# A reordered start: first weights ahead of the activations, the first norm inside the third chunk

## The chip, the cores and the metric

One core of a Trainium2 chip runs the whole program. The metric is the time of one execution on the device in microseconds (us), lower is better. The kernel before took 1706.38 us as the median of three runs (1705.44 to 1707.03).

The engines have their own instruction streams and meet only at semaphores: TensorE (PE in the profile, with its weight loads as PEld), VectorE (DVE), ScalarE (ACT), GpSimd (POOL), and SyncE (SP), which here only issues DMA transfers. Matrix products are written into eight banks of an accumulator memory (PSUM), which the kernel names PS (four banks) and AX (four banks).

## The reference, cut to what matters

The reference is one step of a two-layer streaming encoder over 512 prompt tokens and 32 sample tokens of 1024 features. What this change touches is the very first projection, and the first norm of the memory tokens:

```python
def _rmsnorm(x, g):
    xf = x.astype(jnp.float32)
    y = xf * lax.rsqrt(jnp.mean(xf * xf, axis=-1, keepdims=True) + EPS)
    return (y * g.astype(jnp.float32)).astype(x.dtype)

# layer 0, mixer:
z = _rmsnorm(x, p["g_mix"][l]) @ p["w_in_even"][e]      # (512 + 32, 1024) @ (1024, 2600)
a_b, a_c, a_x, b_q, b_k, b_v, i_q, i_k, i_w = _split(z, EVEN_SIZES)
# ... sparse attention, short convolution, output projection, cross-attention, gated FFN

# memory tokens (256), once per layer:
hm = _rmsnorm(mem, g)
k = _rmsnorm((hm @ w_k).reshape(bsz, m, X_HEADS, X_HEAD_DIM), k_norm)
v = (hm @ w_v).reshape(bsz, m, X_HEADS, X_HEAD_DIM)
```

All of it is float32, and the output has to agree with a float32 reference.

## The kernel before, in words

Everything is held feature-major: a tile is 128 features by 548 token columns (512 prompt, 4 unused, 32 sample), and eight such tiles make up x. To get float32 accuracy from rounded operands, each operand is split in two: a rounded high part (XH, WHI) and the remainder (XL, WLO). A product is then three passes, WHI by XH, WHI by XL and WLO by XH (`product`, L836), each over two halves of 274 columns.

Weights come in **chunks**, 128 output features by all 1024 input features (512 KB, tile WRAW, two buffers used in turn). For each chunk ScalarE rounds WRAW to WHI (`hi`, L448), GpSimd forms WLO = WRAW - WHI (`lo`, L407), and TensorE makes 8 steps (one per input tile, `k`) of six products (`chunk`). VectorE takes the result out of PSUM (`evict`, L1224), and the next chunk but one may then write there. SyncE loads a chunk's weights two chunks ahead, as soon as `lo` of the chunk that last used the buffer is done (semaphore `lo_done`).

The norm is not applied to x. The products run on x times the gain, and each eviction multiplies by RSTD, the reciprocal root of the mean square per token. For it ScalarE squares every x tile (SQ, L462), VectorE sums the eight (SQA, L1207), TensorE multiplies by a matrix of 1/1024 (`mean_square`, L879, into AX banks 0 and 1), ScalarE takes the root (`std`, L473) and VectorE the reciprocal (`rstd`, L1218). So nothing can be evicted before RSTD is there. The memory tokens have the same: a square of the whole 128x2048 tile (MSQ, L525), three halving adds (L1256 to L1258), a product (L926), a root (L534), a reciprocal (RM, L1269) and two transposes (L931) that bring it into RMC.

The first nine chunks of the phase `in_even` are called chunks 0 to 8 below. The order of each engine's instructions is written out by hand, with no planner:

- SyncE: all of the parameters (PR), x tiles 0 and 1, weights of chunk 0, x tiles 2 to 7, constants (CST), weights of chunk 1, CSTB, the memory tokens (MRAW), two small tables, and then, once `lo` of chunk 0 is done, the weights of chunk 2.
- ScalarE: for each x tile the rounding XH and the square SQ in turn; `hi` of chunk 0 after the second tile, `hi` of chunk 1 after the eighth, then MSQ, `hi` of chunk 2, `std`, `hi` of chunk 3.
- VectorE: for each x tile the remainder XL (L1202) and the sum SQA in turn, then the three adds of MSQ, RSTD, the eviction of chunk 0, RM, the evictions of chunks 1 and 2.
- TensorE: chunk 0, `mean_square`, the product of MSQ, chunk 1, chunk 2, the transposes of RM, chunk 3, two small products for the position bias (L937, L938), chunk 4.

From chunk 4 on each chunk has a group of index products of the sparse attention in its middle, and a head norm behind it; VectorE works on scores, head norms and top-k. Chunk 4's middle waits for tables that the steps above produce (`band_vec`, `ki_ready`).

## Time and profile before

| | before |
|---|---|
| median of 3 runs | 1706.38 us |
| the profiled execution's own time | 1706.99 us |
| its span, first to last instruction | 1705.2 us |
| mean granted TensorE clock | 0.982 |
| TensorE busy | 1621.0 us (95%) |
| VectorE, ScalarE, GpSimd busy | 998.2, 637.0, 633.6 us |
| first matrix product | 12.79 us after the span's start |

A timeline row gives the start of a group of like instructions, its length, the engine and line, what it writes and reads, how many there are (x2), and in brackets the idle time of the engine before it and what ended that. Lengths can overlap a little, so the distance from start to start is the safer price of an instruction in a sequence. The kernel is bound by TensorE over most of its length; the edit lies in the first 50 us.

### The profile page before, as it was taken

To read this page: it belongs to the slowest core of one execution; us is meant where nothing else is said; L and a number is where in the kernel's file an instruction comes from. 1 tells how busy PE (TensorE), PEld (TensorE's weight loads), DVE (VectorE), ACT (ScalarE), POOL (GpSimd) and SP (SyncE) were. 2 spreads that over 40 slices of the span, in tenths; PEclk is the share of its full clock that TensorE was granted. 3 is DMA by queue.
4 is the path that set the end of the run, shared out by engine and by line. 5 is a ranking of instruction groups with operands and counts; after the bars stand their busy time and mean duration, and the time that the engine had idled before them with its cause. 6 is when DMAs were issued, how large, how long until landed. Compare 5 with 4: busy or idle time off the path is not lost.

```text
span 1705.2 us, 30940 instructions
## 1 busy us (share of the span) xinstructions
PE 1621.0 (95%) x11888; PEld 1536.8 (90%) x11890; DVE 998.2 (59%) x1300; ACT 637.0 (37%) x960; POOL 633.6 (37%) x305
## 2 busy tenths in 40 slices
PE   5889977998999999999999979899899999999999
PEld 5789843997799999999999979799699999999999
DVE  6799965456355556455656879456646554045530
ACT  5343355335234332233334755333533333123320
...
DMA packets 41714, 153.50 MB, mean 90 GB/s; under 512 B 5344, under 2 KB 5856, under 8 KB 40360
## 3 DMA queue, kind: packets, MB, share of 16 engines
q1 hardware_dynamic: 41640, 152.46, 27.0%
...
q14 instruction: 21, 0.17, 0.0%
...
## 4 chain that ended last, share of the span: by engine, by line
PE 75%; issue 10%; POOL 5%; DVE 5%; ACT 4%; DMA 0%; POOLq 0%; DVEq 0%; SPq 0%; ACTq 0%
PE PS L836 68%; POOL WLO L407 5%; PE AX L1103 2%; DVE RB L1588 1%; PE AX L1012 1%; PE AX L1109 1%; PE AX L896 1%; ACT WHI L448 1%; PE AX L1040 1%; DVE RB L1590 1%; PE PS L1023 1%; ACT LG L632 1%; PE PS L1075 0%; DVE RSTD L1218 0%; DVE SQA L1236 0%
## 5 line engine op out<-in xcount | busy, mean ns | idle before, releaser
L407 POOL TENSOR_TENSOR WLO<-WRAW,WHI 128x1024 fp32r<-128x1024 f32 (+3 forms) x299 | 633.3, 2127 | 1054.1 <-ACT WHI L448 1054.1
L448 ACT ACTIVATE WHI<-WRAW 128x1024 fp32r<-128x1024 f32 (+3 forms) x299 | 268.8, 919 | 721.7 <-PE PS L836 663.6
L836 PE MATMUL PS<-XH,WHI 128*128 128x274 f32 x2256 | 479.9, 294 | 24.9 <-POOL WLO L407 18.4
L836 PE MATMUL PS<-XH,WLO 128*128 128x274 f32 x2256 | 475.7, 292 | 0.0
L836 PE MATMUL PS<-XL,WHI 128*128 128x274 f32 x2256 | 473.2, 291 | 0.0
L836 PEld LDWEIGHTS PS<-XH,WHI 128*128 128x128 f32 x2256 | 361.6, 191 | 33.0 <-POOL WLO L407 18.5
L836 PEld LDWEIGHTS PS<-XL,WHI 128*128 128x128 f32 x2256 | 360.4, 191 | 0.0
L836 PEld LDWEIGHTS PS<-XH,WLO 128*128 128x128 f32 x2256 | 360.0, 191 | 0.0
L836 PE MATMUL PS<-HH,WHI 128*128 128x274 f32 x1216 | 257.3, 293 | 0.7 <-DVE HL L1442 0.7
L836 PE MATMUL PS<-HH,WLO 128*128 128x274 f32 x1216 | 254.6, 291 | 0.0
L836 PE MATMUL PS<-HL,WHI 128*128 128x274 f32 x1216 | 254.4, 291 | 0.0
L836 PEld LDWEIGHTS PS<-HH,WHI 128*128 128x128 f32 x1216 | 194.1, 191 | 2.2 <-DVE HL L1442 1.1
L836 PEld LDWEIGHTS PS<-HL,WHI 128*128 128x128 f32 x1216 | 194.2, 190 | 0.0
L836 PEld LDWEIGHTS PS<-HH,WLO 128*128 128x128 f32 x1216 | 194.1, 191 | 0.0
L1453 DVE TENSOR_TENSOR X<-PS,X 128x548 f32 x56 | 40.8, 729 | 190.9 <-PE PS L836 190.9
L1202 DVE SCALAR_TENSOR_TENSOR XL<-X,PR,XH (+1 forms) x48 | 101.3, 2110 | 53.3 <-ACT XH L461 53.3
L1548 DVE TENSOR_TENSOR HL<-H,HH 128x548 f32 x44 | 87.6, 1992 | 41.0 <-ACT HH L701 41.0
L1539 DVE SCALAR_TENSOR_TENSOR YB<-GB,PR,YB 128x548 f32<-128x548 f32 x44 | 75.5, 1715 | 54.5 <-ACT YB L695 54.5
L1533 DVE TENSOR_TENSOR GB<-PS,RSTD 128x548 f32<-128x548 f32 x44 | 32.0, 728 | 79.6 <-PE PS L836 79.6
L698 ACT ACTIVATE GE<-YB 128x548 f32<-128x548 f32 x44 | 29.1, 662 | 121.2 <-DVE YB L1540 121.2
L1236 DVE RECIPROCAL SQA<-STD 128x548 f32<-128x548 f32 (+1 forms) x17 | 53.5, 3145 | 4.8 <-ACT STD L486 4.5
L1543 DVE TENSOR_TENSOR GE<-GE,RSTD 128x548 f32<-128x548 f32 x44 | 32.1, 730 | 32.0 <-ACT GE L698 32.0
...
## 6 DMA issues: line engine op xcount, KB each, us to landing
WRAW<-in_w_in_even SPq DMA_DIRECT2D x29, 512.0 KB, 3.7
WRAW<-in_w_up0a SPq DMA_DIRECT2D x22, 512.0 KB, 3.6
WRAW<-in_w_up0b SPq DMA_DIRECT2D x22, 512.0 KB, 3.7
WRAW<-in_w_up1a SPq DMA_DIRECT2D x22, 512.0 KB, 3.6
WRAW<-in_w_up1b SPq DMA_DIRECT2D x22, 512.0 KB, 3.6
WRAW<-in_w_mv SPq DMA_DIRECT2D x16, 512.0 KB, 3.6
WRAW<-in_w_xq SPq DMA_DIRECT2D x16, 512.0 KB, 3.6
WRAW<-in_w_xo SPq DMA_DIRECT2D x16, 512.0 KB, 3.7
```

Of the source, the lines that this page charges most:

```text
L407: pool.tensor_tensor(WLO[parity][:, first:last], WRAW[parity][:, first:last], WHIf[parity][:, first:last], ALU.subtract).then_inc(lo_done, ...
L448: act.activation(WHI[parity][:, first:last], WRAW[parity][:, first:last], ACT.Copy).then_inc(hi_done, 2 // len(cuts))
L698: act.activation(GE[:], YB[:], ACT.Gelu_apprx_tanh).then_inc(gelu_done, 1)
L836: ins = pe.matmul(dst, w, x, start=first, stop=last)
L1103: ins = pe.matmul(AX[:, 2 + d, :], MV[:, mb, P * (2 * u + d):P * (2 * u + d) + P], PTX[:, s % 2, mb, :], start=mb == 0, stop=mb == 1)
L1202: dve.scalar_tensor_tensor(XL[:, m, :], X[:, m, :], par(g, m + g0), XHf[:, m, :], ALU.mult, ALU.subtract).then_inc(xl_ready, 1)
L1236: dve.reciprocal(SQA[:, 0:cols], STD[:, 0:cols]).then_inc(std_read, 1)
L1453: dve.tensor_tensor(halves(X[:, m, :]), PS[:, (t0 + k) % 2, :, 0:H], halves(X[:, m, :]), ALU.add).then_inc(evicted, 1)
L1533: dve.tensor_tensor(halves(GB[:, 4:552]), PS[:, t0 % 2, :, 0:H], halves(RSTD[:]), ALU.mult).then_inc(evicted, 1)
L1539: link(dve.scalar_tensor_tensor(YB[:], GB[:, 3:551], par("f_w", f * 3 + (3 * q0 + 1)), YB[:], ALU.mult, ALU.add))
L1543: link(dve.tensor_tensor(GE[:], GE[:], RSTD[:], ALU.mult))
L1548: dve.tensor_tensor(HL[:, f, :], H32[:], HHf[:, f, :], ALU.subtract).then_inc(hl_ready, 1)
```

## The change

What it does, in the order of the engines:

- **SyncE.** The parameters are reordered and loaded in two pieces, a first of 73 columns (eps, the gains and the two cross-attention norms) and later the other 486. The weights of chunk 0 come right behind the first piece, ahead of all of x; the weights of chunk 1 behind x. The weights of chunk 2, with their wait for `lo_done`, move ahead of MRAW and the small tables.
- **Two pieces of the weights' roundings.** Chunks 0 and 1 join the set whose `hi` and `lo` are made in two halves of 512 columns, so TensorE can start a chunk after the first half of `lo`.
- **ScalarE.** A root of one column (WARM) comes first and takes the load of the root's table with it. Then `hi` of chunk 0, all eight XH, `hi` of chunk 1, then the eight SQ with `hi` of chunk 2 behind the third, then MSQ, `std`, `hi` of chunk 3.
- **VectorE.** All eight XL first, then all eight sums. The eviction of chunk 1 moves ahead of RM, that of chunk 2 too, which reads AX instead of PS.
- **TensorE.** Four products on zeros (L937 of the changed kernel, 128x512 in full float32) come first. Chunks 0, 1 and 2 follow one another; chunk 2 writes AX banks 2 and 3 and so waits for no eviction. `mean_square` comes after chunk 2's first step, the product of MSQ after chunk 2, into bank 0. Chunk 3 waits for two evictions, as before. The transposes move behind chunk 3, into bank 1.

```diff
-IN_HALVES = {*range(C0["in_even"] + EVEN_HEAD, C0["mv0"] + 8), *range(C0["odd"], C0["out_odd"] + 2)}
+IN_HALVES = {C0["in_even"], C0["in_even"] + 1, *range(C0["in_even"] + EVEN_HEAD, C0["mv0"] + 8), *range(C0["odd"], C0["out_odd"] + 2)}
...
-            sp.dma_start(PR[:], a["par"]).then_inc(par_landed, 16)
+            sp.dma_start(PR[:, 0:PAR_FIRST], a["par"][:, 0:PAR_FIRST]).then_inc(par_landed, 16)
+            load(0, a["w_in_even"][0], COLS[0], 0)
             for m in range(0, KT, 2):
                 sp.dma_start(X[:, m:m + 2, :], a["x"][:, m:m + 2, :]).then_inc(x_landed[m // 2], 16)
-                if m == 0:
-                    load(0, a["w_in_even"][0], COLS[0], 0)
+            load(1, a["w_in_even"][1], COLS[1], 1)
+            sp.dma_start(PR[:, PAR_FIRST:PAR_COLS], a["par"][:, PAR_FIRST:PAR_COLS]).then_inc(par_rest_landed, 16)
             sp.dma_start(CST[:], a["cst"]).then_inc(cst_landed, 16)
-            load(1, a["w_in_even"][1], COLS[1], 1)
             sp.dma_start(CSTB[:], a["cstb"]).then_inc(cst_landed, 16)
+            load(2, a["w_in_even"][2], COLS[2], 0)
             sp.dma_start(MRAW[:], a["mem"]).then_inc(mem_landed, 16)
             sp.dma_start(OH[:], a["onehot"]).then_inc(bias_in_landed, 16)
             sp.dma_start(RT[:], a["rel"]).then_inc(bias_in_landed, 16)
-            load(2, a["w_in_even"][2], COLS[2], 0)
...
             act.wait_ge(par_landed, 16)
+            act.activation(WARM[:], par("eps"), ACT.Sqrt)
+            hi(0, 0, COLS[0], 0)
             for m in range(KT):
                 if m % 2 == 0:
                     act.wait_ge(x_landed[m // 2], 16)
-                norm_tile(0, m, m % 2)
-                if m == 1:
-                    hi(0, 0, COLS[0], 0)
+                act.activation(XH[:, m, :], X[:, m, :], ACT.Copy, scale=par("g_mix", m)).then_inc(xh_ready, 1)
             hi(1, 1, COLS[1], 0)
+            for m in range(KT):
+                if m >= 2:
+                    act.wait_ge(sq_summed, m - 1)
+                act.activation(SQ[:, m % 2, :], X[:, m, :], ACT.Square).then_inc(sq_ready, 1)
+                if m == 2:
+                    ahead(c0)
+            act.wait_ge(par_rest_landed, 16)
             act.wait_ge(mem_landed, 16)
             act.activation(MSQ[:], MRAW[:], ACT.Square).then_inc(msq_ready, 1)
-            ahead(c0)
             std(0)
             ahead(c0 + 1)
...
-                if not isinstance(t, int) or t >= 2:
+                if not isinstance(t, int) or t >= 3:
                     pe.wait_ge(evicted, t - 1)
...
+                    dst = AX[:, 2:4, :] if isinstance(t, int) and t == THIRD_SLOT else PS[:, slot, :, :]
...
+            pe.wait_ge(warm_in, 1)
+            for i in range(4):
+                ins = pe.matmul(AX[:, 0, :], SQA[:, 0:P], SQA[:, 0:512], start=True, stop=True)
+            ins.then_inc(warm_out, 1)
             even_chunk(0)
+            even_chunk(1)
             pe.wait_ge(cst_landed, 32)
-            mean_square(0)
+            even_chunk(2, {1: lambda: mean_square(0)})
             pe.wait_ge(msum_ready, 1)
-            pe.matmul(AX[:, 2, 0:MEM], ONES_D, MSQ[:, 0, :], start=True, stop=True).then_inc(mssq_mm, 1)
-            even_chunk(1)
-            even_chunk(2)
+            pe.wait_ge(std_ready, 1)
+            pe.matmul(AX[:, 0, 0:MEM], ONES_D, MSQ[:, 0, :], start=True, stop=True).then_inc(mssq_mm, 1)
+            even_chunk(3)
             pe.wait_ge(std_read, 2)
...
-            even_chunk(3)
             pe.wait_ge(bias_in_landed, 32)
-            pe.wait_ge(rmc_ready, 1)
+            pe.wait_ge(evicted, 3)
...
-            zero_sum(0)
+            dve.memset(SQA[:], 0.0).then_inc(warm_in, 1)
             dve.memset(UB[:, 0:4], 0.0)
             dve.wait_ge(par_landed, 16)
+            for m in range(KT):
+                dve.wait_ge(xh_ready, m + 1)
+                dve.scalar_tensor_tensor(XL[:, m, :], X[:, m, :], par("g_mix", m), XHf[:, m, :], ALU.mult,
+                                         ALU.subtract).then_inc(xl_ready, 1)
+            dve.wait_ge(warm_out, 1)
+            for m in range(KT):
+                dve.wait_ge(sq_ready, m + 1)
...
+                dve.tensor_tensor(SQA[:], SQA[:], SQ[:, m % 2, :], ALU.add).then_inc(sq_summed, 1)
+            dve.wait_ge(par_rest_landed, 16)
...
             rstd(0)
             even(0, IQ[:, 0, :])
+            even(1, IQ[:, 1, :])
+            dve.wait_ge(chunk_done, c0 + 3)
+            dve.tensor_tensor(halves(KWB[:]), AX[:, 2:4, 0:H], halves(RSTD[:]), ALU.mult).then_inc(evicted, 1)
             dve.wait_ge(mstd_ready, 1)
             dve.reciprocal(RM[:], STD[:, 0:MEM]).then_inc(std_read, 1)
-            even(1, IQ[:, 1, :])
-            even(2, KWB[:])
```

ScalarE at the head of the program, before (XH and SQ are the high part and the square of an x tile, WHI the high part of a chunk's weights, MSQ the square of the memory tokens, STD the root):

```order
L461 ACTIVATE XH<-X,PR 128x548 [waits sq_summed,x_landed3]
L462 ACTIVATE SQ<-X 128x548
L461 ACTIVATE XH<-X,PR 128x548 [waits sq_summed]
L462 ACTIVATE SQ<-X 128x548
L448 ACTIVATE WHI_57<-WRAW_55 128x1024 [waits raw_landed1]
L525 ACTIVATE MSQ<-MRAW 128x2048 [waits mem_landed]
L448 ACTIVATE WHI_56<-WRAW_54 128x1024 [waits chunk_done,raw_landed0]
L473 ACT_TABLE_LOAD
L473 ACTIVATE STD<-AX,PR 128x548 [waits ssq_done]
L448 ACTIVATE WHI_57<-WRAW_55 128x1024 [waits chunk_done,raw_landed1]
```

And from the last two roundings of x on, now:

```order
L527 ACTIVATE XH<-X,PR 128x548 [waits x_landed3]
L527 ACTIVATE XH<-X,PR 128x548
L452 ACTIVATE WHI_57<-WRAW_55 128x512 [waits raw_landed1]
L452 ACTIVATE WHI_57<-WRAW_55 128x512
L532 ACTIVATE SQ<-X 128x548 x2
L532 ACTIVATE SQ<-X 128x548 [waits sq_summed]
L452 ACTIVATE WHI_56<-WRAW_54 128x1024 [waits chunk_done,raw_landed0]
L532 ACTIVATE SQ<-X 128x548 [waits sq_summed] x5
L537 ACTIVATE MSQ<-MRAW 128x2048 [waits mem_landed,par_rest_landed]
L477 ACTIVATE STD<-AX,PR 128x548 [waits ssq_done]
L452 ACTIVATE WHI_57<-WRAW_55 128x1024 [waits chunk_done,raw_landed1]
```

All squares of x moved behind the weights of chunk 1, the weights of chunk 2 went in among them, and the root went ahead of the weights of chunk 3, with no table load left beside it.

VectorE from the last sums to the evictions, before (IQ is where chunks 0 and 1 go, KWB chunk 2, RM the memory tokens' factor):

```order
L1202 SCALAR_TENSOR_TENSOR XL<-X,PR,XH 128x548 [waits xh_ready]
L1207 TENSOR_TENSOR SQA<-SQA,SQ 128x548 [waits sq_summed,sq_ready]
L1256 TENSOR_TENSOR MSQ<-MSQ 128x1024 [waits msq_ready]
L1257 TENSOR_TENSOR MSQ<-MSQ 128x512 [waits v_step]
L1258 TENSOR_TENSOR MSQ<-MSQ 128x256 [waits v_step]
L1218 RECIPROCAL RSTD<-STD 128x548 [waits std_ready]
L1224 TENSOR_TENSOR IQ<-PS,RSTD 128x548 [waits chunk_done,std_read]
L1269 RECIPROCAL RM<-STD 128x256 [waits mstd_ready]
L1224 TENSOR_TENSOR IQ<-PS,RSTD 128x548 [waits chunk_done]
L1224 TENSOR_TENSOR KWB<-PS,RSTD 128x548 [waits chunk_done]
```

And now:

```order
L1268 SCALAR_TENSOR_TENSOR XL<-X,PR,XH 128x548 [waits xh_ready] x7
L1275 TENSOR_TENSOR SQA<-SQA,SQ 128x548 [waits sq_ready,warm_out]
L1275 TENSOR_TENSOR SQA<-SQA,SQ 128x548 [waits sq_summed,sq_ready] x7
L1277 TENSOR_SCALAR HB<-PR 128x16 [waits par_rest_landed]
L1278 TENSOR_SCALAR GQ<-PR 128x1
L1280 TENSOR_TENSOR MSQ<-MSQ 128x1024 [waits msq_ready]
L1281 TENSOR_TENSOR MSQ<-MSQ 128x512 [waits v_step]
L1282 TENSOR_TENSOR MSQ<-MSQ 128x256 [waits v_step]
L1235 RECIPROCAL RSTD<-STD 128x548 [waits std_ready]
L1241 TENSOR_TENSOR IQ<-PS,RSTD 128x548 [waits chunk_done,std_read]
L1241 TENSOR_TENSOR IQ<-PS,RSTD 128x548 [waits chunk_done]
L1294 TENSOR_TENSOR KWB<-AX,RSTD 128x548 [waits chunk_done]
```

The remainders are a block of their own ahead of the sums, the three adds of MSQ still stand ahead of RSTD, and the second and third evictions passed RM.

## Rows read from the trace of the kernel before

**Rows 1.** Waits of TensorE in the first 60 us: total, times, longest.

```profile
PE PS L836 <- POOL WLO L407: 12.8, 1, 12.8
PE AX L926 <- DVE MSQ L1258: 5.2, 1, 5.2
```

**Rows 2.** Timeline, first 60 us, all engines: start, length, engine, line, what.

```profile
5.49 1.28 ACT L461 ACT_TABLE_LOAD   x1 [5.49 <-DMA X<-in_x]
6.79 0.75 ACT L461 ACTIVATE XH<-X,PR 128x548 fp32r<-128x548 f32 x1
7.45 0.64 ACT L462 ACTIVATE SQ<-X 128x548 f32<-128x548 f32 x1
...
10.38 2.35 POOL L407 TENSOR_TENSOR WLO<-WRAW,WHI 128x1024 fp32r<-128x1024 f32 x1 [9.93 <-ACT WHI L448]
...
10.97 2.34 DVE L1202 SCALAR_TENSOR_TENSOR XL<-X,PR,XH 128x548 fp32r<-128x548 f32 x1 [0.54 <-ACT XH L461]
...
12.79 0.83 PE L836 MATMUL PS<-XH,WHI 128*128 128x274 f32 x2 [12.79 <-POOL WLO L407]
```

**Rows 3.** The same timeline, from the last sum to the first eviction.

```profile
19.24 0.78 DVE L1202 SCALAR_TENSOR_TENSOR XL<-X,PR,XH 128x548 fp32r<-128x548 f32 x1
...
19.94 0.72 DVE L1207 TENSOR_TENSOR SQA<-SQA,SQ 128x548 f32<-128x548 f32 x1
...
20.18 1.89 ACT L525 ACTIVATE MSQ<-MRAW 128x2048 f32<-128x2048 f32 x1
...
20.41 2.48 POOL L407 TENSOR_TENSOR WLO<-WRAW,WHI 128x1024 fp32r<-128x1024 f32 x1 [7.68 <-ACT WHI L448]
...
20.95 1.09 PE L879 MATMUL AX<-SQA,CST 128*128 128x274 f32 x4
...
22.11 1.87 DVE L1256 TENSOR_TENSOR MSQ<-MSQ 128x1024 f32<-128x1024 f32 x1 [1.45 <-ACT MSQ L525]
...
23.16 3.01 POOL L407 TENSOR_TENSOR WLO<-WRAW,WHI 128x1024 fp32r<-128x1024 f32 x1 [0.27 <-ACT WHI L448]
24.00 2.71 DVE L1257 TENSOR_TENSOR MSQ<-MSQ 128x512 f32<-128x512 f32 x1
...
26.75 0.43 DVE L1258 TENSOR_TENSOR MSQ<-MSQ 128x256 f32<-128x256 f32 x1
27.09 3.57 DVE L1218 RECIPROCAL RSTD<-STD 128x548 f32<-128x548 f32 x1
...
30.70 0.73 DVE L1224 TENSOR_TENSOR IQ<-PS,RSTD 128x548 f32<-128x548 f32 x1
```

**Rows 4.** Timeline of TensorE, start and end of chunk 3.

```profile
41.67 0.38 PE L931 MATMUL AX<-CST,RM 128*128 128x128 f32 x2
...
48.12 1.02 PE L937 MATMUL AX<-OH,RT 32*8 32x512 f32 x2
```

**Rows 5.** Windows: stretch, length, busy of PE, PEld, DVE, ACT, POOL, granted clock, DMA share, GB/s.

```profile
2.00:12.00 10.00, 0.00 (x0) 0.00 (x0) 4.03 (x7) 6.50 (x10) 1.62 (x1) 1.00 1.00 378
12.80:16.80 4.00, 4.00 (x17) 4.00 (x18) 4.00 (x7) 2.66 (x5) 0.00 (x0) 1.00 0.99 364
16.80:20.80 4.00, 4.00 (x32) 4.00 (x31) 3.86 (x6) 4.00 (x6) 0.39 (x1) 1.00 0.09 28
```

**Rows 6.** DMA issues at 4.16 and 6.11 us: KB each, us from issue to landing.

```profile
WRAW<-in_w_in_even SPq DMA_DIRECT2D x1, 512.0 KB, 9.8
...
MRAW<-in_mem SPq DMA_DIRECT2D x1, 1024.0 KB, 10.8
```

**Rows 7.** Timeline, 139 to 142 us: halved weights beside a VectorE add of 256 columns.

```profile
139.70 2.73 POOL L407 TENSOR_TENSOR WLO<-WRAW,WHI 128x512 fp32r<-128x512 f32 x2 [0.28 <-ACT WHI L448]
...
140.34 0.95 DVE L1230 TENSOR_TENSOR SQA<-SQ 128x256 f32<-128x256 f32 x1
```

**Rows 8.** Windows, granted clock around two idle times of TensorE, columns as rows 5.

```profile
24.00:26.00 2.00, 0.00 (x0) 0.00 (x0) 2.00 (x1) 1.03 (x2) 2.00 (x1) 0.50 0.83 258
...
28.00:30.00 2.00, 2.00 (x10) 1.91 (x9) 2.00 (x1) 0.00 (x0) 0.00 (x0) 0.50 0.49 197
...
68.00:70.00 2.00, 1.78 (x5) 1.39 (x5) 1.96 (x2) 0.17 (x1) 2.00 (x1) 0.60 0.60 188
```

More of the change, by code:

```diff
@@ L116 @@
 FEEDS = {"out_even": 1, "xo0": 2, "down0b": 3, "out_odd": 4, "xo1": 5}
+THIRD_SLOT = 2
+PAR_FIRST = PAR["bq"][0]
 XUNITS = [0, 1, 2, 4, 3]
@@ L186, in build @@
                   ("FST", [P, FF_T, 4], F32), ("AST", [P, 4, 4], F32), ("CSTATE", [P, 8, 6], F32),
-                  ("HST", [P, 8, 2], F32), ("STAT", [P, 4, 40], F32)]
+                  ("HST", [P, 8, 2], F32), ("STAT", [P, 4, 40], F32), ("WARM", [P, 1], F32)]
         M_AT = C_AT + sum(size(s, d) for _, s, d in consts)
-        RSTD, PR, CST, CSTB, RM, RMC, SP, NSP, SPT, HB, GQ, FST, AST, CSTATE, HST, STAT = pack(C_AT, M_AT, consts)
+        RSTD, PR, CST, CSTB, RM, RMC, SP, NSP, SPT, HB, GQ, FST, AST, CSTATE, HST, STAT, WARM = pack(C_AT, M_AT, consts)
         IDENT, ONES_D, ONES_X, ONES_B = (CST[:, 128 * i:128 * i + 128] for i in range(4))
@@ L533, in _ @@
             std_free(("m", 0))
-            act.activation(STD[:, 0:MEM], AX[:, 2, 0:MEM], ACT.Sqrt, bias=par("eps")).then_inc(mstd_ready, 1)
+            act.activation(STD[:, 0:MEM], AX[:, 0, 0:MEM], ACT.Sqrt, bias=par("eps")).then_inc(mstd_ready, 1)
             for m in range(4):
@@ L843, in chunk @@
                 pe.wait_ge(lo_done, c * 2 + (1 if halved else 2))
-                if not isinstance(t, int) or t >= 2:
+                if not isinstance(t, int) or t >= 3:
                     pe.wait_ge(evicted, t - 1)
                 for k in range(kt):
-                    if halfway is not None and k == kt // 2:
+                    if isinstance(halfway, dict):
+                        if k in halfway:
+                            halfway[k]()
+                    elif halfway is not None and k == kt // 2:
                         halfway()
@@ L854, in chunk @@
                     cut = [slice(0, H), slice(H, T)] if rh.shape[-1] == T else [slice(0, MEM)]
-                    ins = product([PS[:, slot, i, 0:c_.stop - c_.start] for i, c_ in enumerate(cut)],
+                    dst = AX[:, 2:4, :] if isinstance(t, int) and t == THIRD_SLOT else PS[:, slot, :, :]
+                    ins = product([dst[:, i, 0:c_.stop - c_.start] for i, c_ in enumerate(cut)],
                                   WHI[parity][:, w], WLO[parity][:, w], [rh[:, k, c_] for c_ in cut],
@@ L911, in index_group @@
                     pe.wait_ge(kv_landed, 96)
+                    pe.wait_ge(rmc_ready, 1)
                     pe.wait_ge(band_vec, 2)
@@ L1243, in memory_low @@
                                          ALU.subtract).then_inc(ml_ready, 1)
-            zero_sum(0)
+            dve.memset(SQA[:], 0.0).then_inc(warm_in, 1)
             dve.memset(UB[:, 0:4], 0.0)
             dve.wait_ge(par_landed, 16)
+            for m in range(KT):
[5 more added lines that the diff above has]
+                dve.wait_ge(sq_ready, m + 1)
+                if m:
+                    dve.wait_ge(sq_summed, m)
+                dve.tensor_tensor(SQA[:], SQA[:], SQ[:, m % 2, :], ALU.add).then_inc(sq_summed, 1)
+            dve.wait_ge(par_rest_landed, 16)
             dve.tensor_scalar(HB[:], par("ba", 0, 16), 0.5, None, ALU.mult)
             dve.tensor_scalar(GQ[:], par("bq"), float(HD) ** -0.5, None, ALU.mult)
-            for m in range(KT):
-                if m % 2 == 0:
-                    dve.wait_ge(x_landed[m // 2], 16)
-                norm_tile(0, m, m % 2)
             dve.wait_ge(msq_ready, 1)
@@ L1274, in _ @@
             dve.wait_ge(rmt_done, 1)
-            dve.tensor_copy(RMC[:, 0:1], AX[:, 3, 0:1])
-            dve.tensor_copy(RMC[:, 1:2], AX[:, 3, P:P + 1]).then_inc(rmc_ready, 1)
+            dve.tensor_copy(RMC[:, 0:1], AX[:, 1, 0:1])
+            dve.tensor_copy(RMC[:, 1:2], AX[:, 1, P:P + 1]).then_inc(rmc_ready, 1)
             even(3, QT[:, 0, :])
```

9 lines of the change are left out of this document (5 added, 4 removed).

## The prediction

> **What bounds the kernel now.** I read the page first (TensorE 95% busy, so only its idle or slow time can be won), then TensorE's waits in the first 60 us, where the edit lies. There are two big ones [rows 1]: 12.8 us until GpSimd has made the low part of chunk 0, and 5.2 us until VectorE has added up MSQ. The timeline shows what stands behind each.
>
> First wait [rows 2]: x lands at 5.49, a table load takes 1.28, two x tiles are rounded and squared (four instructions), `hi` of chunk 0 starts at 9.19, `lo` at 10.38, and the first product at 12.79. Second wait [rows 3]: `mean_square` is over by about 21.9, but VectorE's three adds run from 22.11 to 27.18. Alone they should take about 2.3 us (1.1 + 0.7 + 0.43). They take 5.1 because the first waits for GpSimd's `lo` of chunk 1 (20.41 + 2.48 = 22.89, and 22.89 + 1.09 is its end, 23.98) and the second, 2.71 instead of 0.7, ends 0.54 after GpSimd's next `lo` (23.16 + 3.01 = 26.17). RSTD is ready at 30.66 and chunk 0 is evicted at 30.70.
>
> In that wait the granted clock falls to 0.50, the 1.2 GHz level: it is there from 24 to 26 us and still from 28 to 30, with ten products in 2 us [rows 8]. The first products on x also come at half pace, 17 in 4 us against 32 in the next 4 [rows 5]. My reference mark is the end of chunk 3: TensorE takes it up behind the transposes at 41.67 and leaves it at 48.12, where the bias product starts [rows 4]. Everything after it hangs on chunks, on what their results feed, and on transfers that wait for these, not on absolute time, so I let the rest shift with this mark.
>
> **The new head, step by step.** Times are on the same clock as the rows.
>
> *Transfers.* From 2 to 12 us they move 378 GB/s [rows 5], so 0.38 MB per us. The weights of chunk 1, issued at 4.16, land 9.8 us later, at 13.96 [rows 6]; with all issued before them 3.84 MB had to move, which was so at 12.1. So landing is the time at which that much has moved plus some 2 us; for the very first transfer of weights, with an empty queue, I take 1.5. In the new order the sums are 0.56 MB with the first weights, 1.12, 1.68, 2.25 and 2.81 MB with the pairs of x, 3.33 with the weights of chunk 1, 4.4 with those of chunk 2 and 5.5 with MRAW. That gives 4.9; 7.0, 8.6, 10.0, 11.5; 12.8; 15.4; 17.7 us.
>
> *Chunk 0.* The table load (1.28) runs from about 3 to 4.3, ahead of the first weights: hidden, if not in the way. `hi` in two pieces 4.9 to 6.0; `lo` in two pieces of about 1.35 (2.73 for two [rows 7]) 5.5 to 8.2. XH of tile 0 is at 7.0 to 7.7. XL of tile 0 has two inputs in on-chip memory beside a running `lo` and behaves as the XL at 10.97, which ended 0.58 after GpSimd [rows 2]: 8.8. So TensorE starts at 8.8 instead of 12.79. XH goes on at 0.66 a tile (6.79 to 7.45 [rows 2]), or as pairs land, and ends at 12.9; XL at 0.70 (19.24 to 19.94 [rows 3]) ends at 13.6. At 2.4 GHz a chunk is 6.2 us (41.67 to 48.12 less the transposes [rows 4]), 0.77 a step, so XL stays ahead and chunk 0 ends at 15.0.
>
> *Chunk 1.* `hi` 12.9 to 14.0, `lo` 13.6 to 14.9 and, with one sum let in between, 15.5 to 16.8. That VectorE gets in between two halves shows in rows 7: the add of 256 columns takes 0.95, not 0.4, ends as GpSimd's first half makes room, and does not wait for the second. TensorE starts on the first half at 15.0 and ends at 21.2 (before: 35.8, since chunk 1 came behind the second wait).
>
> *Squares and sums, which become the critical chain.* Squares start behind `hi` of chunk 1, at 14.0. Sum 0 at 14.9 to 15.5, sum 1 behind `lo` at 16.8 to 17.5. Square 2, then `hi` of chunk 2 16.2 to 17.2, `lo` 17.5 to 19.9. Sum 2 waits for it: 20.5. Five more at 0.70 give 24.0. So the last sum is 3.4 us later than before (20.66). TensorE has made the first step of chunk 2 (22.0) and waits 2 us, makes `mean_square` (1.0 [rows 3]) and the seven other steps: 30.4.
>
> *RSTD.* MSQ's square is done at 25.1 (1.89). The root takes 0.65, `hi` of chunk 3 ends at 26.8, its `lo` asks for the memory at about 27.0. The adds start at 25.2: 1.2 and 0.7 bring the second to 27.1, so the third finds GpSimd waiting already and loses 2.4: 29.8, instead of 27.5. It is a tie within 0.2 us; I take the collision, since the row of before has the same order of events (4.65 or 5.1 us for the three). Reciprocal 3.57 [rows 3] to 33.4, two evictions of 0.66 to 34.8. Chunk 3 waits for two evictions, so it starts at 34.8, while TensorE was ready at 30.9: 3.9 us of idle.
>
> *Clock.* After that idle time the clock may be at 1.2 GHz. The 5.3 us idle brought it there and the return took about 3.2 us of products, a loss of 1.6; after a shorter idle time, 66.4 to 68.2, the clock is at 0.60 in the mean of a window [rows 8], so length alone does not decide. For 3.9 us I take 0.7 of 1.6: 1.1.
>
> *Sum.* Chunk 3 ends at 34.8 + 6.2 + 1.1 = 42.1, the transposes moved behind it add 0.25 [rows 4]: 42.35 against 48.12, a gain of 5.8 us. The profiled execution took 1706.99; it becomes 1701.2, and from the median, 0.6 lower, **1700.6 us**.
>
> **Edits that cost or give nothing in this sum.** The table load ahead of the root at 23 us goes (1.28), but hi and lo of chunk 3 have slack. RM and RMC come later relative to chunk 3, yet RM (1.75 on VectorE) is done by 37 us and the next user is the middle of chunk 4. The rest of the parameters lands by 13.4, asked for at 24. What the order puts in the way: hi of chunk 2 stands among the squares and waits for its weights (15.4 against 16.2, 0.8 us of slack) and for chunk 0; the five squares, MSQ and the root are queued behind it, and a lateness there goes through one for one. MRAW is now issued only after `lo` of chunk 0, with 5.5 us of slack. The bias product's new wait for the third eviction is met at 35.5.
>
> The products on zeros are 2048 columns in full float32. `mean_square`'s 548 columns take 0.91 at 2.4 GHz, so these take 3.4 at the high level and 6.8 at the low; with a rise after 4 us of products, as before [rows 5], they end at 6.9. If they do not hold the clock up until 8.8, chunk 0 ends at 16.7, but TensorE has 2 us idle in chunk 2 and 3.9 behind it, so only hi of chunk 2 feels it, by 0.5. Bounds of this edit: 0 to 0.5 us.
>
> **A rule weighed.** Rows show that the full length of a GpSimd instruction is lost or not at all: 2.71 against 0.7 [rows 3]. The Trainium skill, SBUF — State Buffer, section "Who interferes with whom", says that a VectorE instruction with two inputs in this memory shuts out a GpSimd one that reads it and the other way round, and that whichever is issued first holds it to its end. The trace agrees (2.71 and 3.01 us). By that rule the tie above is worth 2.4 us whole, never a part, and the first rival below follows.
>
> **Rivals.**
> 1. *The third add gets in first.* It needs 0.2 us: for instance `mean_square` at 1.2 GHz after the 2 us idle, which delays the root and with it `lo` of chunk 3. Then RSTD is at 31.1, two evictions at 32.4, idle is under 2 us and the clock stays up: 38.8 with transposes, a gain of 9.3: 1697.1. For it: the tie. Against: before, the second add lost in the same way. 0.25.
> 2. *The zeros do not warm anything.* For: the first 4 us of products ran at half pitch though the profile gives 1.00 for them [rows 5]. Price 0.5 as above: 1701.1. Chance 0.07 (that it shows, beside the main case).
> 3. *The chain is later than I have it.* Weights of chunk 1 or 2 land 1 to 2 us later than 12.8 and 15.4, or one more sum loses to GpSimd (2.4), and the clock falls: gain 2.5 to 3.3, about 1703.5. For: landing times of before spread by 1 us about my rule. 0.14.
> 4. *Slower.* MRAW, now behind a wait and behind all other weights, lands late and the MSQ chain sets RSTD. It decides from a landing at 23.3 on, eats the gain at 29, and costs 3.4 us from 32.5 on; at 34 us the time is 1711. Against: before, in the full queue, it landed 10.8 us after its issue [rows 6], at 16.9, and 18 is what the bytes give now. 0.04.
>
> The main case keeps 0.50, with its own range 1699 to 1702.5 (clock falls or not, 0.5 us for landings). Over all, two tenths left out: 1696.8 to 1703.6. A change of less than 0.2%, 3.4 us, is not to be told from none by a measurement of this kernel; the line is at 1703.0. Faster: 0.48 + 0.25 + 0.06 + 0.03 = 0.82; same 0.14; slower 0.04.
>
> **What would show it.** First weight product on x near 8.8; chunk 0 and 1 without a gap to 21; `mean_square` near 24; the add of 256 columns of MSQ with or without a `lo` in its way; the first eviction near 33.4, chunk 3 from 34.8, bias product at 42.4. Wrong would be: chunk 3 starting at TensorE's own pace (31), a start of the squares much after 14, or a gain at the bias product that is gone by 150 us.

## The result and the profile after

The changed kernel takes 1696.08 us (median of 4 runs, 1695.23 to 1696.79) against 1706.4: the ratio is 0.9939, with a 95% interval of 0.9923 to 0.9954. It is faster, as forecast, but by 10.3 us where I had 5.8, and it lies 0.7 us below my range. Two later measurements of the same kernel gave 0.9963 (0.9948 to 0.9977) and 0.9950 (0.9937 to 0.9963), a gain of 6.3 and 8.5 us by these ratios (7.4 and 8.5 by the medians), so the first was probably a favourable one. The profiled execution has a span of 1693.6 us and took 1695.4.

First TensorE's waits of the changed kernel in the first 60 us (total, times, longest), for [rows 1]:

```profile
PE AX L908 <- ACT SQ L484: 3.2, 2, 1.8
PE AX L891 <- DVE SQA L1275: 2.2, 1, 2.2
PE AX L937 <- DVE SQA L1263: 1.5, 1, 1.5
PE PS L844 <- DVE IQ L1241: 1.3, 1, 1.3
PE PS L844 <- DVE XL L1268: 1.2, 1, 1.2
```

(L908 is the product of a head norm behind the head of the program.) The 12.8 and 5.2 us are gone. What is left at the head is 1.5 ahead of the zeros, 1.2 ahead of the first product on x, 2.2 for the sums and 1.3 for the second eviction.

The timeline of the changed kernel's start, engine by engine (start, length, engine, line, what, idle before), for [rows 2]:

```profile
1.50 6.01 PE L937 MATMUL AX<-SQA 128*128 128x512 f32 x8 [1.50 <-DVE SQA L1263]
8.66 0.49 PE L844 MATMUL PS<-XH,WHI 128*128 128x274 f32 x2 [1.16 <-DVE XL L1268]
...
4.72 1.15 ACT L452 ACTIVATE WHI<-WRAW 128x512 fp32r<-128x512 f32 x2 [1.90 <-DMA WRAW<-in_w_in_even]
...
5.43 2.50 POOL L411 TENSOR_TENSOR WLO<-WRAW,WHI 128x512 fp32r<-128x512 f32 x2 [4.99 <-ACT WHI L452]
12.74 3.56 POOL L411 TENSOR_TENSOR WLO<-WRAW,WHI 128x512 fp32r<-128x512 f32 x2 [4.81 <-ACT WHI L452]
16.95 2.40 POOL L411 TENSOR_TENSOR WLO<-WRAW,WHI 128x1024 fp32r<-128x1024 f32 x1 [0.64 <-ACT WHI L452]
...
13.84 10.26 DVE L1275 TENSOR_TENSOR SQA<-SQA,SQ 128x548 f32<-128x548 f32 x8 [0.42 <-ACT SQ L532]
```

First weights rounded from 4.72 (forecast 4.9), first product on x at 8.66 (8.8), sums from 13.84 (14.9) to 24.10 (24.0). The last agrees only because two errors cancel (see below). Then the timeline around RSTD and the reference mark, for [rows 3, 4]:

```profile
24.15 1.19 PE L891 MATMUL AX<-SQA,CST 128*128 128x274 f32 x4 [2.21 <-DVE SQA L1275]
...
32.41 0.49 PE L844 MATMUL PS<-XH,WHI 128*128 128x274 f32 x2 [1.27 <-DVE IQ L1241]
...
38.92 1.02 PE L954 MATMUL AX<-OH,RT 32*8 32x512 f32 x2
...
25.39 0.72 ACT L477 ACTIVATE STD<-AX,PR 128x548 f32<-128x548 f32 x1 [0.46 <-PE AX L891]
26.00 1.05 ACT L452 ACTIVATE WHI<-WRAW 128x1024 fp32r<-128x1024 f32 x1
...
24.96 1.22 DVE L1280 TENSOR_TENSOR MSQ<-MSQ 128x1024 f32<-128x1024 f32 x1 [0.72 <-ACT MSQ L537]
26.22 0.69 DVE L1281 TENSOR_TENSOR MSQ<-MSQ 128x512 f32<-128x512 f32 x1
26.95 0.43 DVE L1282 TENSOR_TENSOR MSQ<-MSQ 128x256 f32<-128x256 f32 x1
27.29 3.57 DVE L1235 RECIPROCAL RSTD<-STD 128x548 f32<-128x548 f32 x1
...
27.20 2.44 POOL L411 TENSOR_TENSOR WLO<-WRAW,WHI 128x1024 fp32r<-128x1024 f32 x1 [7.85 <-ACT WHI L452]
```

The third add starts at 26.95, GpSimd's `lo` of chunk 3 only at 27.20: no collision. The three adds take 2.4 us where [rows 3] had 5.1. Chunk 3 starts at 32.41, and the mark is at 38.92 instead of 48.12, 9.2 us earlier. That is what my first rival gave (32.4 and 38.8), though not for the cause that it named: in this profile `mean_square` was not slow (1.19 us, granted clock 1.00).

The rest of the gain in this pair of profiles, 11.6 - 9.2 = 2.4 us, comes behind the head. The starts of VectorE's reciprocals in the two traces show it: on the clock of the kernel before, the changed one is 9.2 us ahead up to 71 us, 10.8 from 83 to 211, between 7.5 and 13.8 after that, and 11.6 at the end. The gain at the mark is thus not gone by 150 us, which I had named as a sign of being wrong. The first step is at 71 to 83 us. Windows of the kernel before and of the changed one over the same work just ahead of it (stretch, length, busy of PE, PEld, DVE, ACT, POOL, clock, DMA share, GB/s):

```profile
66.00:72.00 6.00, 4.22 (x18) 3.53 (x16) 5.31 (x7) 2.32 (x3) 2.56 (x1) 0.72 0.54 186
```

```profile
57.00:63.00 6.00, 4.22 (x30) 3.84 (x29) 5.50 (x7) 2.33 (x3) 2.59 (x1) 1.00 0.65 193
```

Before, the clock fell behind the idle time ahead of a head norm and only 18 products fell into the window; the changed kernel has the same idle time (1.78 us in both), 30 products in the window and a granted clock of 1.00. That step alone is 1.6 us. Whether it belongs to the edit is open: the clock fell there in the profiles of the two kernels whose mark stands at 48 (before, and experiment 3), and in none of the three profiles of the changed kernel. The later steps, up and down, I did not trace one by one.

### The profile page after: what moved, and what is told of

Read it like the earlier page. It is cut to its first block, busy times and chain, and to the rows that moved or that the text cites. A ratio compares the mean times of both kernels' runs of the same rounds, so it can differ in the third digit from the quotient of the medians.

```text
span 1693.6 us, 30946 instructions
## 1 busy us (share of the span) xinstructions
PE 1622.5 (96%) x11896; PEld 1534.3 (91%) x11898; DVE 999.3 (59%) x1300; ACT 636.9 (38%) x962; POOL 636.2 (38%) x307
## 4 chain that ended last, share of the span: by engine, by line
PE 75%; issue 10%; POOL 5%; DVE 5%; ACT 3%; DMA 1%; POOLq 0%; SPq 0%; DVEq 0%; ACTq 0%
PE PS L844 67%; POOL WLO L411 5%; PE AX L1120 2%; DVE RSTD L1235 1%; PE AX L1029 1%; PE AX L1057 1%; DVE RB L1613 1%; PE AX L908 1%; PE PS L1040 1%; PE AX L1126 1%; DVE RB L1615 1%; ACT LG L640 0%; ACT WHI L452 0%; DVE SQA L1275 0%; PE PS L1092 0%
## 5 line engine op out<-in xcount | busy, mean ns | idle before, releaser
L844 PE MATMUL PS<-XH,WHI 128*128 128x274 f32 x2240 | 473.4, 293 | 12.4 <-POOL WLO L411 3.4
L844 PE MATMUL PS<-XH,WLO 128*128 128x274 f32 x2240 | 470.4, 291 | 0.0
L844 PE MATMUL PS<-XL,WHI 128*128 128x274 f32 x2240 | 467.8, 290 | 0.0
L844 PEld LDWEIGHTS PS<-XH,WHI 128*128 128x128 f32 x2240 | 356.5, 190 | 21.3 <-issue 12.2
L844 PEld LDWEIGHTS PS<-XL,WHI 128*128 128x128 f32 x2240 | 355.8, 190 | 0.0
L844 PEld LDWEIGHTS PS<-XH,WLO 128*128 128x128 f32 x2240 | 355.5, 190 | 0.0
L1219 DVE SCALAR_TENSOR_TENSOR XL<-X,PR,XH x40 | 93.3, 2333 | 49.0 <-ACT XH L465 49.0
```

The costliest lines, as they stand in the source:

```text
L844: ins = pe.matmul(dst, w, x, start=first, stop=last)
L1219: dve.scalar_tensor_tensor(XL[:, m, :], X[:, m, :], par(g, m + g0), XHf[:, m, :], ALU.mult, ALU.subtract).then_inc(xl_ready, 1)
```

## Experiments

The head of each profile is read by one mark, the start of the bias product (48.1 before, 38.9 in the first profile of the changed kernel); it moves by up to 0.7 us with the landing of the first transfers. A time is a median, a ratio is to runs of the kernel before on the same chip and takes in all runs of both, so it differs from the ratio of the medians by up to 0.0007. Experiments 1 to 4 share their runs of the kernel before, and so do 5 to 8 and 9 to 12. The fences show single rows of a view; rows between them are left out.

**1. The collision, put back.** In the changed kernel, `hi` of chunk 3 goes ahead of the root.

```diff
-            std(0)
             ahead(c0 + 1)
+            std(0)
```

> The changed kernel with two ScalarE instructions exchanged: hi of chunk 3 ahead of the root of the first norm. It makes GpSimd's lo of chunk 3 ask for the memory about 1 us earlier (26.1 us instead of 27.2), so that it stands in the way of the second or third MSQ add. My theory (the third add escaped by 0.25 us, and this collision is worth its full 2.4 us): the last add ends at 29.7 instead of 27.3, RSTD is that much later, chunk 3 starts at 34.7 instead of 32.4, the bias product moves from 38.9 to 41.2, and with a possible fall of the clock to 42.8: 1698.4 us, or 1700 with the clock. Rival (the adds are not what sets RSTD; the root or the sums are): chunk 3 starts at 32.4 to 32.7 as before, 1696.1 to 1696.5 us.

1700.7 us, ratio 0.9961 (0.9948 to 0.9974). The timeline of this run:

```profile
26.71 2.40 POOL L411 TENSOR_TENSOR WLO<-WRAW,WHI 128x1024 fp32r<-128x1024 f32 x1 [5.84 <-ACT WHI L452]
...
26.92 2.74 DVE L1281 TENSOR_TENSOR MSQ<-MSQ 128x512 f32<-128x512 f32 x1
29.70 0.43 DVE L1282 TENSOR_TENSOR MSQ<-MSQ 128x256 f32<-128x256 f32 x1
30.04 3.57 DVE L1235 RECIPROCAL RSTD<-STD 128x548 f32<-128x548 f32 x1
...
35.16 0.49 PE L844 MATMUL PS<-XH,WHI 128*128 128x274 f32 x2 [1.82 <-DVE IQ L1241]
42.86 0.38 PE L949 MATMUL AX<-CST,RM 128*128 128x128 f32 x2
43.17 1.02 PE L954 MATMUL AX<-OH,RT 32*8 32x512 f32 x2
```

The second add takes 2.74 where the changed kernel's took 0.69, the reciprocal starts at 30.04, and chunk 3 takes 7.7 us (35.16 to 42.86) instead of 6.2, at a clock that fell. The mark is 4.25 later than in the first profile: 2.1 for the collision, 0.7 because the sums ended later in this execution (24.80 for 24.10), 1.5 for the clock. The exchange also delays the root, but that is over at 27.17, long before the reciprocal starts behind the third add, so it is not the cause. Of this kernel, my main case was near: 42.35 and 1700.6 forecast, 43.2 and 1700.7 measured. The idle time ahead of chunk 3 was 1.8 us and not 3.9, because the clock had also fallen in chunk 2 (0.54 at 26 to 28 us) and made TensorE late; it fell again all the same.

**2. No products on zeros.**

```diff
-            pe.wait_ge(warm_in, 1)
-            for i in range(4):
-                ins = pe.matmul(AX[:, 0, :], SQA[:, 0:P], SQA[:, 0:512], start=True, stop=True)
-            ins.then_inc(warm_out, 1)
...
-            dve.wait_ge(warm_out, 1)
+            dve.wait_ge(warm_in, 1)
```

> The changed kernel without the four products on zeros. My theory (the idle time in chunk 2 and before chunk 3 hides a slow chunk 0): the first 4 us of products on x run at half pace, chunk 0 ends at 16.4 instead of 14.8, TensorE's wait for the sums in chunk 2 shrinks from 2.2 to about 0.6 us, chunk 3 starts at 32.4 to 32.9, time 1696.1 to 1696.6 us. Rival (the products on zeros are worth the 1.6 us that a warm clock saves): 1697.7 us and the bias product at 40.5.

1695.91 us, ratio 0.9937 (0.9921 to 0.9954): nothing lost. TensorE's timeline:

```profile
9.19 0.80 PE L844 MATMUL PS<-XH,WHI 128*128 128x274 f32 x2 [9.19 <-DVE XL L1264]
24.89 1.19 PE L891 MATMUL AX<-SQA,CST 128*128 128x274 f32 x4 [0.89 <-DVE SQA L1271]
33.14 0.49 PE L844 MATMUL PS<-XH,WHI 128*128 128x274 f32 x2 [1.27 <-DVE IQ L1237]
```

The first two products take 0.80 instead of 0.49, and the next ones come at half the pace, as in the kernel before (its row of 12.8 to 16.8 us in [rows 5]); the profile gives a granted clock of 1.00 for that stretch in both, so it is the pace and not the clock's record that shows it. The wait for the sums shrinks from 2.2 to 0.9 and takes it up; the wait for the second eviction is still 1.27. The mark stands at 39.65, as in the two later profiles of the changed kernel (39.57, 39.64).

**3. TensorE's old order in the changed kernel.** `mean_square` and the product of MSQ are back behind chunk 0, all else as changed.

```diff
             even_chunk(0)
-            even_chunk(1)
             pe.wait_ge(cst_landed, 32)
-            even_chunk(2, {1: lambda: mean_square(0)})
+            mean_square(0)
             pe.wait_ge(msum_ready, 1)
...
+            even_chunk(1)
+            even_chunk(2)
             even_chunk(3)
```

> The changed kernel with TensorE's old order of the norm: mean_square and the product of MSQ right behind chunk 0, chunks 1 and 2 behind them (chunk 2 still in AX). Loads, roundings, sums and zeros stay as in the changed kernel. My theory (the gain comes from work that fills the wait for RSTD, not from the earlier first product): mean_square still waits for the sums at 24, the product of MSQ for 27.4, chunk 1 starts at 28, at 1.2 GHz for some 3 us after the long idle time, and the bias product stands at 48, as in the kernel before: 1705 to 1707 us. Rival (the earlier first product at 8.7 is the gain): 4 us of it are kept, the bias product at 44 and 1702 us.

1708.09 us, ratio 1.0009 (0.9999 to 1.0019): the gain is gone, all of it.

```profile
8.77 0.49 PE L844 MATMUL PS<-XH,WHI 128*128 128x274 f32 x2 [0.70 <-DVE XL L1269]
24.50 2.16 PE L891 MATMUL AX<-SQA,CST 128*128 128x274 f32 x4 [8.85 <-DVE SQA L1276]
27.68 1.22 PE L944 MATMUL AX<-MSQ,CST 128*128 128x256 f32 x2 [1.02 <-DVE MSQ L1283]
48.53 1.02 PE L955 MATMUL AX<-OH,RT 32*8 32x512 f32 x2
```

The first product starts 4 us earlier than in [rows 2] and TensorE then stands idle for 8.85 us until the sums are there, and comes back at 1.2 GHz (granted clock 0.50 from 20 to 28 us). This does not test the earlier product by itself: the changed order of roundings and squares also ends the sums 3.7 us later than before (24.35 for 20.66). The weights loaded early with the squares in their old places were not run.

**4. One line moved in the kernel before.** The product of MSQ goes behind chunk 1.

```diff
             mean_square(0)
+            even_chunk(1)
             pe.wait_ge(msum_ready, 1)
             pe.matmul(AX[:, 2, 0:MEM], ONES_D, MSQ[:, 0, :], start=True, stop=True).then_inc(mssq_mm, 1)
-            even_chunk(1)
             even_chunk(2)
```

> The kernel before with one line moved: the product of MSQ goes behind chunk 1 on TensorE instead of ahead of it. My theory: chunk 1 starts at 22.9, when its lo is done, instead of 27.9, ends at 29.1, chunk 2 then waits for the eviction of chunk 0 until 31.4, the clock perhaps stays up, and the bias product moves from 48.1 to 44.0 or 44.5: 1702 us. Rival (VectorE's chain absorbs it: RM and the evictions come later by as much): bias product at 47 to 48, 1705.5 us or more.

1702.48 us, ratio 0.9971 (0.9961 to 0.9981), mark at 44.14, as expected. The wait for MSQ of [rows 1] is gone; a new one of 1.86 us stands ahead of chunk 2, for the eviction of chunk 0:

```profile
22.83 0.53 PE L836 MATMUL PS<-XH,WHI 128*128 128x274 f32 x2 [0.91 <-POOL WLO L407]
29.06 0.59 PE L927 MATMUL AX<-MSQ,CST 128*128 128x256 f32 x2
31.52 0.49 PE L836 MATMUL PS<-XH,WHI 128*128 128x274 f32 x2 [1.86 <-DVE IQ L1224]
...
44.14 1.02 PE L937 MATMUL AX<-OH,RT 32*8 32x512 f32 x2
```

**5. All of TensorE's order, with the third slot, in the kernel before.** Loads, roundings and squares as before. VectorE's evictions of chunks 1 and 2 go ahead of RM with it; the diff shows TensorE's waits and order only.

```diff
-                if not isinstance(t, int) or t >= 2:
+                if not isinstance(t, int) or t >= 3:
                     pe.wait_ge(evicted, t - 1)
...
             mean_square(0)
+            even_chunk(1)
+            even_chunk(2)
             pe.wait_ge(msum_ready, 1)
...
+            even_chunk(3)
             pe.wait_ge(std_read, 2)
...
```

> The kernel before with only TensorE's part of the change: chunks 1 and 2 right behind the first mean_square, chunk 2 in AX banks 2 and 3 without a wait for an eviction, the product of MSQ behind chunk 2, the transposes behind chunk 3, the evictions of chunks 1 and 2 ahead of RM. Loads, roundings, squares, halves and the start stay as in the kernel before, and there are no products on zeros. My theory (the reorder gives somewhat more than half of the gain, the earlier start the rest): chunk 1 from 22.9, chunks 1 and 2 without a gap to 35.3, chunk 3 at 35.9 with no wait for its two evictions (32.1), bias product at 42.4 against 48.1 and 38.9: gain 5.7, 1700.7 us. Rival (the third slot adds nothing to moving the product of MSQ alone): bias product at 44.1 and 1702.4 us as in that run.

1698.36 us, ratio 0.9963 (0.9949 to 0.9977), a gain of 6.3 us. The mark stands at 41.96 (42.4 expected):

```profile
35.08 0.59 PE L931 MATMUL AX<-MSQ,CST 128*128 128x256 f32 x2
41.65 0.38 PE L935 MATMUL AX<-CST,RM 128*128 128x128 f32 x2
41.96 1.02 PE L940 MATMUL AX<-OH,RT 32*8 32x512 f32 x2
```

6.2 of the 9.2 us at the mark need no change of loads or roundings (0.2 of them because the transfers landed earlier in this execution: first product at 12.55 for 12.79). Chunk 3 starts at 35.32 without a wait. Experiment 3 shows the other side: those without this order give nothing. In time, the third slot's share over experiment 4 is not shown (the intervals overlap), and neither is what the loads and roundings add: the changed kernel beside this one (experiment 8) has the same ratio, 0.9963, and a median 0.7 us lower.

**6. Chunks 0 and 1 rounded whole.** `IN_HALVES` as before, all else as changed.

> The changed kernel with chunks 0 and 1 rounded whole again instead of in two halves. My theory (halves let a sum of VectorE in between and start chunk 1 early, but TensorE's waits behind hide the latter): lo of chunk 1 ends later by some 0.5 us, the first sum waits for all of it, the last sum comes 0.5 to 1 us later, bias product at 39.4 to 40: 1696.6 to 1697.1 us. Rival (worth nothing): 1696.1. Second rival: the shift makes the third MSQ add meet lo of chunk 3, +2.4 and perhaps the clock: 1699 to 1700.

1695.67 us, ratio 0.9952 (0.9933 to 0.9971). The first product on x comes at 9.58, the mark at 40.03, 0.4 to 1.1 us later than in the three profiles of the changed kernel, as expected. The time is not the 1696.6 to 1697.1 that I expected, and 2.0 us below the changed kernel beside it (experiment 8), with intervals that overlap: whether the halves are worth anything in time is not shown. The third add started at 28.06 and `lo` at 28.31: again 0.25 apart.

**7. RSTD ahead of the adds.**

```diff
-            dve.wait_ge(msq_ready, 1)
-            link(dve.tensor_tensor(MSQ[:, 0:4, :], MSQ[:, 0:4, :], MSQ[:, 4:8, :], ALU.add))
...
             rstd(0)
             even(0, IQ[:, 0, :])
             even(1, IQ[:, 1, :])
+            dve.wait_ge(msq_ready, 1)
+            link(dve.tensor_tensor(MSQ[:, 0:4, :], MSQ[:, 0:4, :], MSQ[:, 4:8, :], ALU.add))
...
-            even_chunk(3)
+            even_chunk(3, {3: memory_square})
...
```

> The changed kernel with RSTD and the first two evictions ahead of the three MSQ adds on VectorE, the product of MSQ moved from behind chunk 2 to behind the third step of chunk 3, hi of chunk 4 ahead of the memory tokens' roundings, and their remainders behind the bias tables. It takes away the adds, and so the collision that I had expected, from the path to RSTD. My theory (RSTD is set by the adds, 27.3 instead of 26.1): reciprocal at 26.1, chunk 3 at 31.1 instead of 32.4, bias product at 37.7, 1694.9 us, and no execution with the 2.4 us collision, so less spread. Rival (what is won at chunk 3 is lost in chunk 4, whose middle waits for the bias tables and whose lo comes later): bias product at 37.7 but the first head norm no earlier, 1696.1 us.

1696.26 us, ratio 0.9951 (0.9936 to 0.9965); the changed kernel beside it (experiment 8) 1697.68. The reciprocal starts at 27.01 instead of 27.88, yet the mark is 39.42 against 39.57. My expectation of 37.7 was wrong, and the windows of this run say why:

```profile
24.00:26.00 2.00, 1.42 (x5) 1.12 (x5) 0.67 (x3) 1.36 (x1) 0.00 (x0) 0.80 0.00 0
26.00:28.00 2.00, 2.00 (x10) 1.98 (x9) 0.99 (x1) 1.66 (x2) 0.00 (x0) 0.50 0.00 0
```

The clock fell in the wait for the sums, the first 3 us of chunk 2 ran at 1.2 GHz, and TensorE came to chunk 3 at 32.5, later than the evictions, which were over at 31.99. Sums that ended 0.4 us later than in the first profile (24.52) and the slower `mean_square` (1.64 us) account for the reciprocal at 27.01 instead of 26.1.

**8 and 12. The changed kernel again**, among the runs of two later sets.

> The changed kernel itself, once more, for its spread and beside the others on the same chip. Theory: 1696.1 us, bias product at 38.9 or up to 0.8 later with the landings, and most executions without the collision of the third add; if the collision is a tie of 0.25 us that landings decide, some executions stand at 1698.5 to 1700.7. Rival (the order of add and lo is fixed by data dependences, since both hang on the same squares): no execution above 1697.5.

> The changed kernel once more, on the same chip as these. Theory: 1696 to 1697.7 us, bias product at 38.9 to 39.6, and no execution at 1699 or above unless the clock fell more often; the third MSQ add stays ahead of lo of chunk 3 by 0.2 us or more, since both hang on the same squares and sums.

1697.68 us, 0.9963 (0.9948 to 0.9977), and 1696.5 us, 0.9950 (0.9937 to 0.9963). Marks 39.57 and 39.64. `mean_square` and the two instructions that race, in the timeline of run 8 and then of run 12:

```profile
24.75 1.71 PE L891 MATMUL AX<-SQA,CST 128*128 128x274 f32 x4 [1.89 <-DVE SQA L1275]
...
27.54 0.42 DVE L1282 TENSOR_TENSOR MSQ<-MSQ 128x256 f32<-128x256 f32 x1
...
28.30 2.40 POOL L411 TENSOR_TENSOR WLO<-WRAW,WHI 128x1024 fp32r<-128x1024 f32 x1 [7.54 <-ACT WHI L452]
```

```profile
24.75 2.16 PE L891 MATMUL AX<-SQA,CST 128*128 128x274 f32 x4 [2.35 <-DVE SQA L1275]
...
27.54 0.42 DVE L1282 TENSOR_TENSOR MSQ<-MSQ 128x256 f32<-128x256 f32 x1
...
28.76 2.40 POOL L411 TENSOR_TENSOR WLO<-WRAW,WHI 128x1024 fp32r<-128x1024 f32 x1 [8.81 <-ACT WHI L452]
```

In both, the clock fell (0.50 at 26 to 28 us) and `mean_square` took 1.71 and 2.16 us instead of 1.19, so the root and `lo` come later and the add has 0.76 and 1.22 us to spare. With experiments 2, 6 and 10 and the first profile of the changed kernel that makes six profiles with this order of root and `hi`, and the add is ahead in all: by 0.25 (three times), 0.76, 1.15 and 1.22. In the profiles it was no tie. A profile shows one execution, though. Of the six in experiment 8, three took longer than the 1697.5 us that my rival allowed, and two of them, 1698.93 and 1699.45, lie where I had put the collision. They have no trace. The mean granted clock of the first, 0.984, is no lower than the 0.983 of the profiled one at 1697.04, so falls of the clock are not an obvious reason for it. That the collision happens in some executions is not excluded.

**9. Squares first.** Experiment 7, with `hi` of chunk 2 in halves and behind all squares, the root ahead of the square of MSQ, and `mean_square` between chunks 1 and 2. The diff is against the changed kernel and leaves out what experiment 7 has too.

```diff
                 act.activation(SQ[:, m % 2, :], X[:, m, :], ACT.Square).then_inc(sq_ready, 1)
-                if m == 2:
-                    ahead(c0)
+            ahead(c0)
+            std(0)
...
-            even_chunk(2, {1: lambda: mean_square(0)})
+            mean_square(0)
+            even_chunk(2)
```

> The run with RSTD ahead of the MSQ adds, carried on: all eight squares ahead of hi of chunk 2 (so that no lo of 2.4 us stands among the sums), chunk 2 in two halves, mean_square between chunks 1 and 2, the root ahead of MSQ. My theory (the start is bound by the chain of sums, which loses 2.4 us to lo of chunk 2): last sum at 22 instead of 24.1 to 24.7, mean_square 22 to 23, chunk 2 from 23.4 to 29.6, RSTD and two evictions done at 28.8, chunk 3 from 29.6 with no wait, bias product at 36.1 to 36.8 instead of 38.9 to 39.6: 1693 to 1694 us where the changed kernel stands at 1696 to 1697.5. Rival (the clock falls in the wait before mean_square and takes half of it back): bias product at 37.5 to 38, 1695 to 1696 us.

1695.41 us, ratio 0.9937 (0.9925 to 0.9950), the changed kernel beside it 1696.5 and 0.9950. The eight sums (VectorE) and TensorE's timeline:

```profile
14.95 7.64 DVE L1278 TENSOR_TENSOR SQA<-SQA,SQ 128x548 f32<-128x548 f32 x8
```

```profile
22.75 1.16 PE L890 MATMUL AX<-SQA,CST 128*128 128x274 f32 x4 [0.52 <-DVE SQA L1278]
...
36.99 1.02 PE L957 MATMUL AX<-OH,RT 32*8 32x512 f32 x2
```

The sums take 7.6 instead of 10.3 us, since no whole `lo` stands among them, and the mark is at 36.99, 2.65 us ahead of experiment 12's. The mark misses the 36.1 to 36.8 that I expected by 0.2 us, the time the 1693 to 1694 by 1.4. In the time 1.1 us of the 2.65 is seen, with intervals that overlap: a better version at the head, not shown to be one over the whole kernel.

**10. `mean_square` behind the fifth step of chunk 2**, in the changed kernel (`{1:` becomes `{5:`).

> The changed kernel with mean_square behind the fifth step of chunk 2 instead of the first. TensorE then has work until the sums are there. My theory (chunk 3 waits for RSTD's chain, not for TensorE): the 2 us wait inside chunk 2 goes and comes back ahead of chunk 3, bias product within 0.7 us of the changed kernel's, time the same; with one idle time of some 3 us instead of two the clock may fall in chunk 3, up to 1.6 us slower. Rival (TensorE's wait in chunk 2 is on the path): 1.5 to 2 us faster.

1698.79 us, ratio 0.9964 (0.9951 to 0.9976), mark at 40.92.

```profile
25.66 1.09 PE L891 MATMUL AX<-SQA,CST 128*128 128x274 f32 x4
32.90 0.70 PE L844 MATMUL PS<-XH,WHI 128*128 128x274 f32 x2 [3.43 <-DVE IQ L1241]
```

The wait ahead of `mean_square` goes and stands ahead of chunk 3, 3.43 instead of 1.27 us. Chunk 3 starts no earlier, the clock fell (0.50 at 34 to 36 us), and chunk 3 takes 7.7 us instead of 6.2, near the 1.6 that I had allowed for. The median is 2.3 us above that of the changed kernel beside it, with intervals that overlap.

**11. Experiment 9 without the zeros.**

> The run with the squares first, without the products on zeros. There TensorE has little idle time left to hide a slow start. My theory: chunk 0 at 1.2 GHz costs 1.6 us, of which the wait ahead of mean_square (about 0.7 us) hides a part, so the bias product comes 0.5 to 1.6 us later and the time is 0.5 to 1.6 us longer than with the zeros. Rival (products on zeros are worth nothing here too): same time within 0.3 us.

1694.83 us, ratio 0.9938 (0.9924 to 0.9952). The mark is at 37.44, 0.45 later, below what I expected: TensorE comes to `mean_square` 1.0 us later, and the wait of 0.52 us takes up half of that. The time shows no difference. I cannot show that the zeros are worth anything in either form.

## Why the prediction was wrong

**The transfers and chunks 0 and 1: right.** 8.66 for 8.8, chunk 1 over at 21.0 for 21.2.

**The sums: right by luck.** 24.10 for 24.0, but `lo` of chunk 2 was over at 19.35 and not at 19.9, and the sums behind it came every 0.83 us, not every 0.70: the last four squares start at 19.96, 20.80, 21.63 and 22.47, each behind the sum that frees its buffer. My sum had no such wait.

**"I take the collision": the step that failed.** The forecast had the third add ask 0.1 us behind GpSimd; it was ahead by 0.25. Two small terms were off in opposite directions. The adds began at 24.96, not 25.2 (MSQ's square was done earlier), and the root at 25.39, not 25.1, since `mean_square` started at 24.15 and took 1.19 us where I had 24.0 and 1.0. Each is within 0.3 us, as good as the other terms; but two sums were compared with a margin of 0.1, and I gave the side that lost twice the chance. What the step cost: chunk 3 started at 32.41 and not at 34.8, 2.4 us for the add, and with it went the idle time of 3.9 us (1.27 measured) and the 1.1 us for a clock that did not fall there. Together they are, to 0.1, the 3.4 us between 42.35 and 38.92. The argument from the kernel before did not carry: there `hi` followed MSQ at once, as experiment 1 has it again, and here the root lies between. That order stood in the lists of both kernels. Price and mechanism were right: 2.1 us in experiment 1 where I had 2.4, with 1.5 for the clock behind it.

**What I had as chance was, in the profiles, structure.** Add and `lo` hang on the same squares, and whatever slows `mean_square` delays only `lo`, away from the collision. The three profiles with `mean_square` behind the first step and the clock up have the same 0.25 us, though their sums ended at 24.10, 24.83 and 25.21, and in all six the add is ahead. What could bring the collision back is a late square of MSQ; no profile has one, and the two long executions of experiment 8 stay open.

**"Everything after it shifts with this mark": right in the mean, not in one profile.** The shift was 9.2 at the mark and 11.6 at the end. One fall of the clock behind a short idle time, in the kernel before only, is 1.6 us of the difference, and neither my sum nor its range had such falls. So the measured 1696.08 came out 1.0 below even the rival's 1697.1 and outside the range; this part is chance or unexplained, and not the mechanism that I forecast. In the later sets the marks gave 8.5 and the times 6.3 and 8.5, both below the rival's 9.3.

**The zeros: right.** 0 to 0.5 forecast, none found; they do bring the first products on x to full pace (0.49 for 0.80 us), which my second rival doubted. **The table load and MRAW: hidden,** as forecast; the sum needed neither. (By my own rule MRAW's landing was 18.3 and not 17.7 us; the slack of 5 us covers it.)

**The source of the gain.** My text counted the earlier start as a step of the sum. Experiments 3 to 5 put it in order: one moved line gives 4.0 of the 9.2 us at the mark, the rest of TensorE's order with the third slot 2.2 more, and the new loads and roundings give nothing without this order. With it they move the mark by another 2.3 to 3.0. In experiment 5 chunk 3 starts without a wait, so TensorE's own work is on the path and an earlier start shortens it, until in the changed kernel the chain of sums and RSTD ends last again (1.27 us of wait ahead of chunk 3). In time those 3 us are not shown.
